# Gathered rows added at keys 9 to 117, eight of them asked for ahead of the values, and the first 32 tokens ended in mid-stage

## The reference

```
q = (xn @ w_q);  s = q . sub_keys;  16 best of each side, 16 best of the 256 sums -> expert ids, softmax gates
hid = einsum('td,ted->te', x, u_tab[ids])                 # 128 picks per token
out = einsum('te,ted->td', gelu(hid) * gate, v_tab[ids])
y   = RMSNorm(h + out) * final_norm_w
```

## Time and profile before

| | us |
|---|---|
| median of 3 runs (lowest, highest) | 2195.39 (2193.57, 2197.99) |
| the profiled execution | 2195.33 |
| its span, first to last instruction | 2193.5 |
| TensorE busy | 2109.4 |
| VectorE busy | 1319.1 |
| ScalarE busy | 869.8 |
| GpSimd busy | 983.9 |

### The profile page before, as it was taken

How to read it: one execution, slowest core, us unless ns; L and a number is a source line. 1 busy time by engine, 2 the same in 40 slices (tenths; PEclk the granted TensorE clock), 3 DMA queues, 4 the chain that set the end, 5 groups by cost and what they waited for, 6 DMA issues and landing times.

```text
span 2193.5 us, 41955 instructions
## 1 busy us (share of the span) xinstructions
PE 2109.4 (96%) x16647; PEld 2054.5 (94%) x16647; DVE 1319.1 (60%) x2502; ACT 869.8 (40%) x1693; POOL 983.9 (45%) x619
## 2 busy tenths in 40 slices
PE   8997898898999999999999999999999999999997
PEld 7996787788999999999999999999999999999996
DVE  4564656667778988699811111111257787777776
ACT  5334455543333333499832222222233333333332
POOL 1433344422254554411133333333367787777620
PEclk9999999999999999999999999999999999999998
DMA  3447267625465666477776767676669999999972
GB/s 129 179 137 218 88 190 222 189 81 184 137 197 191 192 194 198 131 210 224 224 256 237 253 219 237 239 250 215 221 239 337 336 336 340 339 339 330 334 267 77
DMA packets 302135, 488.98 MB, mean 223 GB/s; under 512 B 34400, under 2 KB 226720, under 8 KB 301832
## 3 DMA queue, kind: packets, MB, share of 16 engines
q1 hardware_dynamic: 273800, 402.55, 55.5%
q0 software_dynamic: 28160, 83.99, 11.1%
HBM read 395.61 MB, written 157.50 MB: 252 GB/s over the span
## 4 chain that ended last, share of the span: by engine, by line
PE 71%; DVE 2%; ACT 1%; DMA 1%; issue 1%; SPq 0%; POOL 0%; DVEq 0%; ACTq 0%; POOLq 0%
PE banks L130 22%; PE banks L131 22%; PE banks L132 22%; PE banks L2299 4%; PE banks L1975 1%; DMA u_raw<-arg_u 1%; DVE n_y L349 0%; DMA scratch_hid<-gelu_ahead 0%; SPq L2163 0%; DVE res_x L2846 0%; DVE res_lo L356 0%; DVE n_sq L390 0%; DVE n_inv L342 0%; DVE gates_in L2853 0%; DVE gates_in L2843 0%
## 5 line engine op out<-in xcount | busy, mean ns | idle before, releaser
L130 PE MATMUL banks<-res_hi,u_high 128*128 128x288 f32 x1456 | 438.4, 301 | 4.2 <-POOL u_low L2172 3.2
L132 PE MATMUL banks<-res_hi,u_low 128*128 128x288 f32 x1456 | 429.6, 295 | 0.0
L131 PE MATMUL banks<-res_lo,u_high 128*128 128x288 f32 x1456 | 429.6, 295 | 0.0
L130 PE MATMUL banks<-w_high,v_high 128*128 128x416 f32 x1024 | 360.0, 352 | 0.3 <-DVE w_low L2727 0.3
L131 PE MATMUL banks<-w_low,v_high 128*128 128x416 f32 x1024 | 359.3, 351 | 0.0
L132 PE MATMUL banks<-w_high,v_low 128*128 128x416 f32 x1024 | 357.2, 349 | 0.0
L2172 POOL TENSOR_TENSOR u_low<-u_raw,u_high 128x1024 fp32r<-128x1024 f32 x75 | 179.9, 2399 | 306.0 <-ACT u_high L2168 306.0
L2734 DVE TENSOR_TENSOR gated<-gelu_out,gates_in 128x416 f32<-128x416 f32 x76 | 44.9, 592 | 418.9 <-ACT gelu_out L2688 385.4
L130 PEld LDWEIGHTS banks<-res_hi,u_high 128*128 128x128 f32 x1456 | 274.2, 188 | 4.9 <-POOL u_low L2172 3.7
L131 PEld LDWEIGHTS banks<-res_lo,u_high 128*128 128x128 f32 x1456 | 274.2, 188 | 0.1
L132 PEld LDWEIGHTS banks<-res_hi,u_low 128*128 128x128 f32 x1456 | 273.8, 188 | 0.0
(11 more groups left out here) (443 smaller groups left out, 4535.0 us busy)
## 6 DMA issues: line engine op xcount, KB each, us to landing
scratch_v_rows<-arg_v SPq DMA_DIRECT2D x128, 512.0 KB, 7.5
v_raw<-scratch_v_rows SPq DMA_DIRECT2D x128, 512.0 KB, 6.1
u_raw<-arg_u SPq DMA_DIRECT2D x37, 1024.0 KB, 5.7
scratch_gates<-gate_stage SPq DMA_DIRECT2D x13, 2048.0 KB, 9.4
scratch_prod<-gated SPq DMA_DIRECT2D x128, 208.0 KB, 3.3
w_raw<-scratch_prod SPq DMA_DIRECT2D x128, 208.0 KB, 5.0
q_raw<-arg_u SPq DMA_DIRECT2D x38, 512.0 KB, 3.9
gates_in<-scratch_gates SPq DMA_DIRECT2D x19, 832.0 KB, 5.0
```

The lines of the kernel that those rows point to most:

```text
L130: pe.matmul(out, ah, bh, start=first, stop=False)
L131: pe.matmul(out, ah, bl, start=False, stop=False)
L132: return pe.matmul(out, al, bh, start=False, stop=last)
```

## The change

Four edits. The rows are due at keys 9 to 117, not 10 to 122; by `rows_due` the first eight are then due at keys 9, 10, 11, 11, 12, 13, 13, 14 (before: 10, 11, 12, 12, 13, 14, 14, 15), and the last at 116 (121). FOLD_KEY moves from 36 to 34. GpSimd asks for rows 0 to 7 first, then for values 0 to 15, then for row s and value s+8 in turn. The 32 tokens of the first part are ended in mid-stage by a new function `finish_rest` on VectorE after key 43, with their root on ScalarE after key 40 and their four stores on SyncE at key 47; `finish_rows` ends only the other 128.

```
-ACC_FROM, ACC_TO = 10, 122
+ACC_FROM, ACC_TO = 9, 117
...
+                if k == FOLD_KEY + 13:
+                    r = rest_y.rearrange("p (d j t) -> p d j t", j=4, t=32)
+                    sp.wait_ge(row_scaled, 3)
+                    for b in range(REST // 32):
+                        for j in range(4):
+                            sp.dma_start(a["y"][32 * j:32 * j + 32, :, P + 32 * b:P + 32 * b + 32],
+                                         r[32 * b:32 * b + 32, :, j, :]).then_inc(stored, 16)
...
         def sp_last(sp):
...
-            sp.wait_ge(row_scaled, 4)
-            for b in range(REST // 32):
-                for j in range(4):
-                    sp.dma_start(a["y"][32 * j:32 * j + 32, :, P + 32 * b:P + 32 * b + 32], r[32 * b:32 * b + 32, :, j, :]).then_inc(
-                        stored, 16)
-            sp.wait_ge(row_scaled, 5)
+            sp.wait_ge(row_scaled, 6)
...
                 split_v_high(act, k)
                 split_w_high(act, k)
+                if k == FOLD_KEY + 6:
+                    act.wait_ge(row_squared, 1)
+                    act.activation(stat[0:REST, 4:5], stat[0:REST, 3:4], ACT.Sqrt, bias=core.eps[0:REST, 0:1],
+                                   scale=1.0 / D_MODEL).then_inc(row_rooted, 1)
             act.wait_ge(row_squared, 2)
-            act.activation(stat[0:REST, 4:5], stat[0:REST, 3:4], ACT.Sqrt, bias=core.eps[0:REST, 0:1], scale=1.0 / D_MODEL)
             act.activation(stat[:, 1:2], stat[:, 0:1], ACT.Sqrt, bias=core.eps[:, 0:1], scale=1.0 / D_MODEL).then_inc(
...
+            dve.wait_ge(row_rooted, 2)
+            link(dve.reciprocal(stat[:, 2:3], stat[:, 1:2]))
+            dve.tensor_scalar(total[:, :], total[:, :], stat[:, 2:3], None, ALU.mult).then_inc(row_scaled, 1)
+            dve.wait_ge(row_scaled, 4)
+            dve.transpose(ring[:, 1, :], total[:, :]).then_inc(row_scaled, 1)
+            dve.wait_ge(row_scaled, 5)
+            y4 = sparse_y.rearrange("p (d j t) -> p d j t", j=4, t=32)
+            dve.tensor_tensor(y4, y4, bc(norm_b[:, :, :].rearrange("p j d -> p d j"), 3, [P, DT, 4, 32]),
+                              ALU.mult).then_inc(row_scaled, 1)
+
+        def finish_rest(dve):
+            link = core.chains["dve"].on(dve)
+            sums = rest_total[0:REST, :]
             dve.wait_ge(row_rooted, 1)
+            link(dve.reciprocal(stat[0:REST, 5:6], stat[0:REST, 4:5]))
             dve.tensor_scalar(sums, sums, stat[0:REST, 5:6], None, ALU.mult).then_inc(row_scaled, 1)
             dve.wait_ge(row_scaled, 1)
+            dve.transpose(rest_y, sums).then_inc(row_scaled, 1)
             dve.wait_ge(row_scaled, 2)
...
                 if k == FOLD_KEY + 3:
                     fold_rest(dve)
+                if k == FOLD_KEY + 9:
+                    finish_rest(dve)
             finish_rows(dve)
...
+            for s in range(CHUNK // 2):
+                row(s)
             for s in range(CHUNK):
                 value(s)
-            for s in range(COLS):
+            for s in range(CHUNK // 2, COLS):
                 row(s)
-                if s + CHUNK < COLS:
-                    value(s + CHUNK)
+                if s + CHUNK // 2 < COLS:
+                    value(s + CHUNK // 2)
```

More of the change, by code:

```diff
@@ L2595, in sp_out @@
                         sp.dma_start(fold[:, q - 1, :], rest_total[q * REST:(q + 1) * REST, :]).then_inc(fold_in, 16)
+                if k == FOLD_KEY + 13:
[5 more added lines that the diff above has]
+                                         r[32 * b:32 * b + 32, :, j, :]).then_inc(stored, 16)
         def sp_last(sp):
             q = sparse_y.rearrange("p (d j t) -> p d j t", j=4, t=32)
-            r = rest_y.rearrange("p (d j t) -> p d j t", j=4, t=32)
-            sp.wait_ge(row_scaled, 4)
-            for b in range(REST // 32):
-                for j in range(4):
-                    sp.dma_start(a["y"][32 * j:32 * j + 32, :, P + 32 * b:P + 32 * b + 32], r[32 * b:32 * b + 32, :, j, :]).then_inc(
-                        stored, 16)
-            sp.wait_ge(row_scaled, 5)
+            sp.wait_ge(row_scaled, 6)
             for b in range(4):
@@ L2790, in finish_rows @@
             dve.tensor_reduce(stat[:, 0:1], ring[:, 0, :], AX_X, ALU.add).then_inc(row_squared, 1)
+            dve.wait_ge(row_rooted, 2)
[10 more added lines that the diff above has]
+            sums = rest_total[0:REST, :]
             dve.wait_ge(row_rooted, 1)
-            dve.reciprocal(stat[0:REST, 5:6], stat[0:REST, 4:5])
-            link(dve.reciprocal(stat[:, 2:3], stat[:, 1:2]))
-            sums = rest_total[0:REST, :]
+            link(dve.reciprocal(stat[0:REST, 5:6], stat[0:REST, 4:5]))
             dve.tensor_scalar(sums, sums, stat[0:REST, 5:6], None, ALU.mult).then_inc(row_scaled, 1)
-            dve.tensor_scalar(total[:, :], total[:, :], stat[:, 2:3], None, ALU.mult).then_inc(row_scaled, 1)
             dve.wait_ge(row_scaled, 1)
-            link(dve.transpose(rest_y, sums))
+            dve.transpose(rest_y, sums).then_inc(row_scaled, 1)
             dve.wait_ge(row_scaled, 2)
-            dve.transpose(ring[:, 1, :], total[:, :]).then_inc(row_scaled, 1)
             dve.wait_ge(norm_in, 64)
@@ L2803, in finish_rows @@
             dve.tensor_tensor(r4, r4, bc(norm_b[0:REST, :, :].rearrange("p j d -> p d j"), 3, [REST, DT, 4, 32]),
[L2804 to L2807, removed]
                               ALU.mult).then_inc(row_scaled, 1)
```

## The result

The changed kernel takes **2215.05 us** (median of 6 runs, 2212.70 to 2226.91) beside 2195.83 of the kernel before in the same set (6 runs, 2190.51 to 2200.30): ratio 1.0079, 95% interval 1.0055 to 1.0102. It is slower by 17.3 us by that ratio, where 10.1 was forecast. The profiled execution took 2214.13 (span 2212.0), 18.8 more than that of before.

What follows compares the result with a forecast made beforehand. The prediction took TensorE, busy without a gap in the output stage, to bound the kernel. A stall of 10.4 plus 2.2 of lower clock less 2.5 at the end gave +10.1 on 2195.39: 2205.5 us, range 2201.5 to 2211.

Steps and rivals of the forecast that it cites:

- The first stall: Before key 10: values 0 to 15 wait behind rows 0 to 7, so TensorE stalls 10.4 us (bounds 9.0 to 14.6).
- The clock: After the stall before key 10: TensorE restarts at the lower clock level and loses 2.2 us.
- Part 2: Chunks after the first, with rows at keys 9 to 117 and values 8 ahead: no cost, 0 us.
- Covered with 2.0 to spare: Chunk 1's weighing in key 20's turn: VectorE done at 1701.3, before key 21's start at 1703.3, so nothing reaches TensorE.
- It still keeps up, barely: GpSimd's pace in the stage: a row and a value cost 3.02 us, one row due per 3.06.
- later chunks gain 0.6 each: Weighings after chunk 1: each chunk gains 0.6 us on the 2.0 to spare at key 21.
- Part 3: Finish of the first 32 tokens in key 43's turn: 3.3 us of VectorE work, covered, 0 us; at most 3.3.
- Part 4: The end: VectorE's chain loses 3.1 us of work, of which 2.5 is gained (bounds 0 and 3.1).
- The gap before the sum: At the end, TensorE's idle time before the sum matmul: some 1.3 us in place of 3.77.
- (a): Rival at the first values: gathers go at 1.51 us and landing is slow, +14.3, 2209.7 us; chance 0.20.
- (c): Rival at key 10: the eight rows don't hold the values, only the end's 2.5 is gained, 2192.8 us; chance 0.07.
- (b): Rival: chunk 1 at key 20 or the finish at key 43 also stalls, 1.3 to 3.3 us more, some 2207.8; chance 0.11.

Runs made afterwards that it cites:

- order_alone: The kernel before with GpSimd's new order alone, rows at keys 10 to 122 and the old finish: 2216.09 us, ratio 1.0062.
- rows_ungated: The changed kernel with rows asked for up to 16 keys ahead instead of 8: 2206.35 us, ratio 1.0024.
- ahead_8: The changed kernel with values 0 to 15 asked for first, then rows 0 to 7, later values still 8 ahead: 2201.26 us, ratio 1.0002.
- values_first: The changed kernel with GpSimd's old order (16 values, then row s and value s+16), all else as changed: 2201.06 us, ratio 0.9999.
- fill_one: The kernel before with an added one-input VectorE reduction in keys 12 to 115; this and fill_two, one run each: 2212.52 and 2214.83 us.
- fill_two: The kernel before with an added two-input VectorE addition in keys 12 to 115; this and fill_one, one run each: 2212.52 and 2214.83 us.
- narrow_adds: The changed kernel with each gathered row added over 16 of its 1024 columns, but for the two first rows: 2220.10 us, ratio 1.0011.
- wide_again: The changed kernel with rows at keys 10 to 122 again, a second time: 2218.58 us, ratio 1.0014.
- after_wide: The changed kernel with rows at keys 10 to 122 again: 2217.12 us, ratio 1.0023.
- finish_alone: The kernel before with the mid-stage finish of the 32 tokens alone, keys 10 to 122 and old order: 2208.22 us, ratio 0.9977.
- finish_again: The kernel before with the mid-stage finish of the 32 tokens alone, a second time: 2213.81 us, ratio 0.9996.

## Why the prediction failed, step by step

**The first stall: right in mechanism, 2.9 too large.** Row 7 was forecast at 1623.0, value 15 at 1644.3, landed 1648.5. The trace:

```profile
1620.19 0.94 POOL L2880 DMA_INDIRECT row_ring<-scratch_v_rows,expert_of_pick  x1 [2.34 <-PE banks L132]
1621.43 0.95 POOL L2870 DMA_INDIRECT value_of_pick<-scratch_hid,hidden_of_pick  x1 [0.30 <-issue]
...
1640.59 0.94 POOL L2870 DMA_INDIRECT value_of_pick<-scratch_hid,hidden_of_pick  x1 [0.30 <-issue]
```

```profile
1642.85 0.17 DVE L2761 TENSOR_TENSOR weight_of_pick<-value_of_pick,gate_of_pick 128x16 f32<-128x16 f32 x1 [17.12 <-DMA value_of_pick<-scratch_hid,hidden_of_pick]
```

The stage began 2.9 earlier, so value 15 is 0.8 early by the stage's own time (row 7 took 0.94 where I had 1.33, and no gather up to value 15 took more than 1.35). The landing took 2.26, not the 4.2 that I took, and not the 3.8 that was my bound, the least of the loaded trace. The two make 2.7 of the 2.9. The Trainium skill, "DMA: Bandwidth & Descriptors", section "Anatomy of one DMA — SWDGE (gpsimd) path", has about 2.0 for a small transfer; by that the prediction had 8.2, and 7.55 was measured. The trace comes within 0.3 of the page where the queues are quiet (DMA share 0.02 while value 15 is under way), and not elsewhere (median 5.6).

**The clock: 2.2 forecast, 1.5 here.** Windows after the first stall, then after the second large one:

```profile
1646.00:1648.00 2.00, 2.00 (x7) 1.90 (x7) 2.00 (x3) 0.00 (x0) 1.64 (x2) 0.50 0.69 152
1648.00:1650.00 2.00, 2.00 (x11) 1.96 (x10) 1.90 (x3) 0.00 (x0) 1.70 (x2) 0.82 1.01 389
...
1755.00:1760.00 5.00, 5.00 (x19) 4.85 (x20) 4.90 (x5) 0.00 (x0) 4.09 (x3) 0.71 0.83 272
```

TensorE is at the lower level (1.2 GHz, 0.50) for some 3 us after each, less than the 3.6 to 5.4 of the earlier trace rows. Other kernels of this case do have that much: 5.0 us after the wait of 7.64 in order_alone (2.4 lost) and 5.6 after one of 4.14 in rows_ungated (2.6 lost). So 2.2 was a fair value, and 1.5 is what this trace happened to have.

**The step that failed: Part 2, "later chunks and the tighter spacing ... I take 0".** It cost 12.2 of waits, 1.4 for the tails and restarts of six, and 1.4 of clock: 15.1 us. Two sentences of it were wrong, and one thing it didn't look at, the landing of one value, is the largest piece.

*"Covered with 2.0 to spare."* For chunk 1 the pace was right: from value 15 to value 31 are 32 gathers in 1688.90 - 1640.59 = 48.3, that is 1.51 each. So was the work between weighing and key 21's operands, 3.3. But key 21 was due at 1697.0, not 1703.3: 2.9 of that is the stage's earlier start, the rest that the first stall and its clock took less. GpSimd, which isn't held by that stall, had its value only 3.2 earlier (weighed 1694.92, I had 1698.1). The 2.0 to spare became a wait of 1.16. I had sized a margin from a stall that I had overestimated. At the low end of my own range, a stall of 7.7 and 1.8 of clock, the same sum has 0.2 too little.

*"It still keeps up, barely"*, 3.02 against 3.06, and "later chunks gain 0.6 each". It doesn't. The 128 pairs from value 31 to value 159 take 392.8 us in the kernel before, 3.07 each, of which 0.03 is waits for keys and the like. With rows due at keys 9 to 117 they take 3.10 (ahead_8), 3.12 (rows_ungated), 3.15 (values_first, where no weighing waits) and 3.16 (the changed kernel), and next to nothing of that is waits. So the pace that I had read off one pattern of three is over 3.06 in every order. After a wait VectorE has a queue of work and no idle time, and the gathers slow down, as nearly all of them begin inside one of its two-input instructions. GpSimd while VectorE stands still, and then while it catches up:

```profile
1687.66 0.94 POOL L2880 DMA_INDIRECT row_ring<-scratch_v_rows,expert_of_pick  x1 [0.30 <-issue]
1688.90 0.94 POOL L2870 DMA_INDIRECT value_of_pick<-scratch_hid,hidden_of_pick  x1 [0.30 <-issue]
...
1696.39 1.99 POOL L2870 DMA_INDIRECT value_of_pick<-scratch_hid,hidden_of_pick  x1 [0.30 <-issue]
1698.68 1.39 POOL L2880 DMA_INDIRECT row_ring<-scratch_v_rows,expert_of_pick  x1 [0.30 <-issue]
1700.37 1.08 POOL L2870 DMA_INDIRECT value_of_pick<-scratch_hid,hidden_of_pick  x1 [0.30 <-issue]
1701.76 1.33 POOL L2880 DMA_INDIRECT row_ring<-scratch_v_rows,expert_of_pick  x1 [0.30 <-issue]
```

Four in 5.0 us become four in 7.0, 1.75 each. From value 31 to value 159 (1688.90 to 2093.98) 128 pairs take 405.1; at full speed of TensorE they are due in 128 * 3.06 = 391.7. The 13.4 between the two is close to what TensorE lost from key 22 on (11.1 of waits, 1.2 around them, 1.4 of clock: 13.7). The pace alone doesn't make this loss: values_first has nearly the same one and TensorE waits 3.0 in all, as there the values are asked for 16 rows ahead and none comes late. Nor is all of it GpSimd's doing, as TensorE's stalls also hold back the keys that its rows wait for: it is a circle of three engines, and the experiments break it at three points. Without the late start 6.4 us are left of 24.4 (ahead_8), at the looser spacing 11.3 (order_alone), with values 16 ahead 4.0 (values_first). fill_one and fill_two show one link by itself, a VectorE without idle time slowing GpSimd. narrow_adds was to cut that link and did so in part.

The largest piece has a source of its own. The second large wait, 6.74 at 1755.00, with its tail and clock 8.4 of the 15.1, lies behind value 47, which took 10.35 to land, the slowest of the 160; with the median of 5.6 the wait would be near 2. Value 47 is issued at 1739.98, right behind the three copies of 128 KB by which SyncE brings the quarters of the 32 tokens together ahead of `fold_rest`:

```profile
1736.86 2.33 SPq L2595 DMA_DIRECT2D gates_early<-gelu_out  x3
```

They take 7.7 to 11.7 to land. From 1740 to 1745 the queues are busy 1.04 and move 256 GB/s, where the earlier trace rows have 337 at 0.96. In every trace of this case it is 212 to 293 GB/s at a share of 0.98 to 1.05 from 5 to 10 us after the first copy. The slow values stand there too. In the kernel before, the three slowest (8.8, 8.4 and 7.8) are issued 2 to 7 us after the first copy, in values_first the four slowest from 0.6 before to 8.4 after it. Value 47 is issued 1.9 after it in ahead_8 and rows_ungated and takes 8.8 and 9.0, which gives their only waits of TensorE over 1 us (3.95 and 4.14); it is issued 0.7 before it in order_alone and takes 7.8, and 5.5 and 6.3 before it in wide_again and after_wide, where it takes 5.0 and 5.6. Two traces don't fit: in narrow_adds it is issued 7.1 before and takes 7.4, and ahead_8 has four slow values (8.0 to 10.2) at the stage's start, far from the copies. No run moved the copies alone, so this is a reading of traces and not shown by an experiment. But it was there to be asked before: I had the longest landing of before (8.8) and used the median, without looking at what stood beside the long ones, and the change itself moves FOLD_KEY and with it the copies.

**Part 3, the finish in mid-stage: right.** It runs from 1802.7 to 1806.1; the nearest waits of TensorE lie 48 us before and 146 us after it, and neither finish_alone nor finish_again has one on VectorE there.

**Part 4, the end: 2.5 forecast, 3.0 measured.** The gap before the sum was forecast at 1.3 and is 1.27, against 3.77. The other 0.5 is in what I called unchanged: in the kernel before TensorE falls to the lower level during the sum that follows the 3.77 (clock 0.74 from 2179.6 to 2181.8), and after the gap of 1.27 it doesn't (1.00), so the last two matmuls take 0.86 in place of 1.35. VectorE does wait for TensorE's last block:

```profile
2197.43 0.59 DVE L2848 TENSOR_TENSOR res_x<-banks,res_x 128x416 f32<-128x416 f32 x1 [0.42 <-PE banks L132]
```

**The rivals.** (a), the gathers at 1.51 with a slow landing, fell: all but one of the sixteen took 0.94 or 0.95, that is 1.25 from start to start, and the last landed in 2.3. (c), that nothing reaches TensorE, fell. (b), that later weighings stall too, is what happened, priced at 1.3 to 3.3 where it was 15.1: I counted it as one more stall at one place, and it came at six. With the first stall as measured (7.55 + 0.24 + 1.5 = 9.3) less 3.0, the forecast would have been +6.3; by the profile the rest of the +18.5 is 15.1 from (b) and -2.9 from the stage's earlier start. (The low end of the range, 2201.5, is 0.3 under its own terms, 7.7 less 1.3 on 2195.4.)

## What to carry over

When a gather queue is put a little behind, ask not only whether the first wait is covered but what the engines do while they catch up: a pace measured beside an engine with 23% of idle time doesn't hold once that idle time is gone, and a balance of 3.02 against 3.06 is no margin. Before a row that waits for a milestone is put ahead of work that waits for nothing, count in the code when the milestone falls: the wait of row 7, not its gathers, made the first stall. A margin that depends on an earlier term of the same sum has to be tried at both bounds of that term. And where a spread of landings goes from 3.8 to 8.8, look at what else is under way beside the longest before the median is used: a late value that falls beside it costs the most.

## What the runs showed of the hardware

- A gather of 128 values lands 2.3 us after its start with few loads in flight (2.23 to 2.33 in six kernels, each time value 15 of the new order), and in 3.2 to 10.3 in the loaded stage, with medians of 5.4 to 5.7.
- A gather takes 0.94 us and the next starts 0.30 later, unless it begins inside a VectorE instruction with two SBUF inputs: then it ends 0.82 after that instruction (156 of the 158 gathers over 1.0 us of before end so behind some instruction; 1649 of 1649 that begin well inside a two-input one are held in the 13 traces). With one input it depends: a 32x1024 transpose held none of nine, a 128x1024 product with a scalar all seven, a 32x1024 reduction the one.
- So the pace depends on how the two streams meet, and VectorE's busy share alone doesn't give it: from 1690 to 1890 the kernel before has a gather every 1.54 us with VectorE 80% busy, the changed kernel one every 1.61 with 81%, the two with an added instruction 1.70 and 1.72 with 95%.
- Waits of TensorE of 0.7 to 1.4 us left its clock alone (granted clock 1.00). After 3.95, 4.14, 6.74, 7.55 and 7.64 it restarted at the lower level and stayed there for 3.3, 5.6, 2.9, 3.1 and 5.0 us, which cost 1.4 to 2.6; the longer wait didn't cost more.
- From 5 to 10 us after the first of three copies of 128 KB from SBUF to SBUF the queues move 212 to 293 GB/s at a share of 0.98 to 1.05 in all 13 traces, where the kernel before has 337 at 0.96 on average late in the stage. In five of the six traces that show landings the slowest gather of a value stands beside them (7.8 to 10.3).
- In two of three sets of runs TensorE had 4 to 14 us of gaps, mostly around keys 7 to 14, that no wait explains, in all seven kernels profiled there, and the kernel before, timed but not profiled there, took 11 to 14 us more. In both traces of the new order in these sets, with VectorE waiting 17.1 as in the first, 0 and 0.9 us of the first stall reached TensorE. The medians fit a smaller cost of the order there, but don't prove it: 15.5 us over the kernel without it in the first set, 8.9 and 4.8 in the other two, with 0.2 to 0.3% (4 to 7 us) of interval on each ratio.
